# A hybrid-attention and mixture-of-experts layer: gathered rows placed eight partitions apart, expert weights in a ring of six landing pieces and five split pieces

## What is computed

```
scores = sigmoid(xf @ w_router)                    # 512 tokens, 64 experts
idx    = top 8 experts of each token (4 of 8 groups allowed)
wts    = chosen scores / their sum * 2.5
routed = sum over the 8 experts of  wts * (silu(x @ w_gate[e]) * (x @ w_up[e])) @ w_down[e]
shared = (silu(x @ w_gate_s) * (x @ w_up_s)) @ w_down_s
out    = layer_norm(ALPHA * x + shared + routed)
```

## Time and profile before

| | |
|---|---|
| three runs | 1386.76, 1387.98, 1388.95 us; median 1387.98 |
| the profiled execution | 1387.71 us, its span 1385.9 us |
| PE busy | 1311.4 us (95%), 6084 instructions |
| DVE busy | 894.1 us (65%) |
| ACT busy | 709.2 us (51%) |
| POOL busy | 402.5 us (29%) |
| DMA | 311.36 MB, 66971 packets |
| chain that ended last | PE 69%, DMA 22%, ACT 4%, DVE 3% |
| loads of expert weights | 192 x 1 MB, median 11.3 us (gate, up) and 10.8 us (down) from issue to landing |
| gathers, scatters | 64 and 64, median 10.8 us and 9.0 us from issue to landing |

### The profile page before, as it was taken

How to read it: one execution, slowest core, us unless ns; L and a number is a source line. 1 busy time by engine, 2 the same in 40 slices (tenths; PEclk the granted TensorE clock), 3 DMA queues, 4 the chain that set the end, 5 groups by cost and what they waited for, 6 DMA issues and landing times.

```text
span 1385.9 us, 15960 instructions
## 1 busy us (share of the span) xinstructions
PE 1311.4 (95%) x6084; PEld 974.1 (70%) x6084; DVE 894.1 (65%) x1163; ACT 709.2 (51%) x863; POOL 402.5 (29%) x266
## 2 busy tenths in 40 slices
PE   7999999999979999998999999999999999999955
PEld 4989886666656676455587877777777777777722
DVE  4001116655665656465488888888888888888858
ACT  4222323333323321002378888888888888887710
POOL 3232312212232343127233332322222222233204
PEclk9999999999999999998999999999999999999987
DMA  4732201211111151503599999999999999999594
GB/s 161 260 100 74 69 20 57 75 40 39 58 38 58 63 211 38 221 28 125 177 388 359 377 377 363 376 366 369 368 369 371 362 369 373 369 369 373 224 373 180
DMA packets 66971, 311.36 MB, mean 225 GB/s; under 512 B 17660, under 2 KB 17788, under 8 KB 40400
## 3 DMA queue, kind: packets, MB, share of 16 engines
q1 hardware_dynamic: 47408, 276.64, 53.7%
q0 software_dynamic: 19488, 33.70, 6.4%
HBM read 305.74 MB, written 42.01 MB: 251 GB/s over the span
## 4 chain that ended last, share of the span: by engine, by line
PE 69%; DMA 22%; ACT 4%; DVE 3%; issue 1%; POOL 0%; POOLq 0%; SPq 0%; DVEq 0%; ACTq 0%
DMA raw<-in_w_gu 20%; PE PS L651 18%; PE PS L896 9%; PE PS L846 4%; PE PS L849 4%; PE PS L843 4%; PE PS L759 4%; PE PS L707 4%; PE PS L777 4%; ACT w_hi_e L1120 3%; PE PS L730 3%; PE PS L718 2%; DMA parts<-y_d 2%; PE PS L828 2%; PE PS L680 2%; PE PS L679 2%
## 5 line engine op out<-in xcount | busy, mean ns | idle before, releaser
L1436 DVE TENSOR_TENSOR w_lo_e<-raw,w_hi_e 128x2048 fp32r<-128x2048 f32 x192 | 433.8, 2282 | 4.1 <-ACT w_hi_e L1120 4.0
L1120 ACT ACTIVATE w_hi_e<-raw 128x2048 fp32r<-128x2048 f32 x192 | 368.4, 1919 | 113.8 <-DMA raw<-in_w_gu 75.1
L1655 POOL DMA_INDIRECT y_d<-y_slots,tab x64 | 114.2, 1785 | 426.3 <-PE PS L915 284.6
L1607 POOL TENSOR_TENSOR w_lo<-ring,w_hi 128x1024 fp32r<-128x1024 f32 x54 | 128.3, 2376 | 325.7 <-ACT w_hi L1027 325.7
L1280 DVE CUSTOM_DVE_ANT_0 region<-PS,region 128x128 f32<-128x128 f32 (+1 forms) x64 | 30.6, 477 | 183.0 <-PE PS L707 180.9
L846 PE MATMUL PS<-w_hi_e,xs_lo 128*128 128x512 f32 x512 | 144.1, 403 | 0.0
L843 PE MATMUL PS<-w_hi_e,xs_hi 128*128 128x512 f32 x512 | 143.8, 402 | 0.0
L849 PE MATMUL PS<-w_lo_e,xs_hi 128*128 128x512 f32 x512 | 138.7, 393 | 0.0
L1071 ACT ACTIVATE region<-region,nmax 128x128 f32<-128x128 f32 (+3 forms) x80 | 43.6, 546 | 149.7 <-DVE nmax L1280 149.4
L846 PEld LDWEIGHTS PS<-w_hi_e,xs_lo 128*128 128x128 f32 x512 | 91.9, 188 | 32.6 <-DVE xs_lo L1462 15.1
L849 PEld LDWEIGHTS PS<-w_lo_e,xs_hi 128*128 128x128 f32 x512 | 96.1, 188 | 22.3
(11 more groups left out here) (181 smaller groups left out, 2169.5 us busy)
## 6 DMA issues: line engine op xcount, KB each, us to landing
raw<-in_w_gu SPq DMA_DIRECT2D x128, 1024.0 KB, 11.3
raw<-in_w_down_e SPq DMA_DIRECT2D x64, 1024.0 KB, 10.8
ring<-in_w_merge SPq DMA_DIRECT2D x32, 640.0 KB, 3.9
parts<-y_d SPq DMA_DIRECT2D x8, 1536.0 KB, 16.5
ring<-in_w_proj SPq DMA_DIRECT2D x22, 512.0 KB, 3.5
region<-in_w_out SPq DMA_DIRECT2D x1, 4096.0 KB, 14.1
parts<-y_d SPq DMA_DIRECT2D x4, 1024.0 KB, 20.4
bias_d<-bias_rows SPq DMA_DIRECT2D x3, 1280.0 KB, 11.1
```

The source lines that it names most:

```text
L1120: nc.scalar.activation(w_hi_e[b][:, lo:hi], raw[b][:, lo:hi], ACT.Copy).then_inc(made, 1)
L1436: nc.vector.tensor_tensor(w_lo_e[b][:, lo:hi], raw[b][:, lo:hi], w_hi_e[b][:, lo:hi].bitcast(F32), ALU.subtract).then_inc(made, 1)
L1607: nc.gpsimd.tensor_tensor(wl, w, wh.bitcast(F32), ALU.subtract).then_inc(w_lo_made, 1)
L1655: pool.indirect_dma_start(y_d, bass.IndirectOffsetOnAxis(ap=rows, axis=0), y_slots[:, b, :], None, bounds_check=last_row, oob_is_err=False ...
```

## The change

1. **Slots.** The table is read so that slot s = 16 i + j lands in partition 8 j + i (i 0 to 7, j 0 to 15): consecutive slots are eight partitions apart. With 64 tokens, the partitions 8 j + 0 to 8 j + 3 of all 16 j are used. Nothing else of gather and scatter is changed.
2. **Landing.** The 192 pieces of expert weights have one order (`WEIGHTS`: a0 b0 a1 b1 d0 a2 b2 d1 ...; piece n) and land in a ring of six (`LANDED`): four in `raw`, two in the memory of `xT`. `raw` is no longer the memory of `w_lo_e`. From piece 6 on, piece n is loaded once DVE has made the low part of piece n - 6. Pieces 0 and 1 are loaded right behind the shared expert's weights, before the stores of `x1`; pieces 2 and 3 once the shared expert's gate and up are done (they read `xT`); 4 and 5 once `base` has finished (their place is that of `x1`) and `x1` is stored.
3. **Split parts.** `w_hi_e` and `w_lo_e` are rings of five pieces (`SPLIT`). ACT's high of piece n waits for the piece n - 5 to be used by PE.

PE, ACT and DVE keep their order of work.

```diff
+PIECE = GU // 2
+LANDED = 6
+SPLIT = 5
+LAND_AT = (0, 1, 4, 5, 2, 3)
+SPLIT_AT = (0, 4, 1, 2, 3)
+def weight_pieces():
+    order = [("a", 0), ("b", 0)]
+    for e in range(1, N_EXP):
+        order += [("a", e), ("b", e), ("d", e - 1)]
+    return order + [("d", N_EXP - 1)]
...
+        def landing(n):
+            at = LAND_AT[n % LANDED]
+            if at < 4:
+                return raw[:, at, :]
+            return xT[:, :, :].rearrange("p a b -> p (a b)")[:, (at - 4) * PIECE:(at - 3) * PIECE]
...
-            def load_first(e):
-                sp.dma_start(raw[e % 2][:, 0:PART], a["w_gu"][e][:, 0:PART]).then_inc(p0_in[e % 2], 16)
...
+            def load(n):
+                what, e = WEIGHTS[n]
+                if n in (2, 3):
+                    sp.wait_ge(gu_b, QT)
+                elif n in (4, 5):
+                    sp.wait_ge(based, 2 * QT)
+                    sp.wait_ge(x1_stored, 16 * QT)
+                elif n >= LANDED:
+                    sp.wait_ge(lo_made, n - LANDED + 1)
...
+                sp.dma_start(landing(n), weights).then_inc(piece_in[n % LANDED], 16)
...
+            load(0)
+            load(1)
             store_x1(0)
             store_x1(1)
-            sp.wait_ge(mix_done, QT)
-            load_first(0)
-            load_second(0)
-            load_down(0)
             store_x1(2)
             store_x1(3)
...
-            for e in range(1, N_EXP):
-                sp.wait_ge(gu_a, e + QT - 1)
-                load_first(e)
-                sp.wait_ge(gu_b, e + QT - 1)
-                load_second(e)
-                if e >= 2:
-                    sp.wait_ge(y_done, e + QT - 2)
-                    load_down(e - 1)
-            sp.wait_ge(y_done, N_EXP + QT - 2)
-            load_down(N_EXP - 1)
+            for n in range(2, len(WEIGHTS)):
+                load(n)
...
+            def high(what, e):
+                n = PIECE_NO[what, e]
+                act.wait_ge(piece_in[n % LANDED], 16 * (n // LANDED + 1))
+                if n >= SPLIT:
+                    used, by = WEIGHTS[n - SPLIT]
+                    act.wait_ge({"a": gu_a, "b": gu_b, "d": y_done}[used], by + QT + 1)
+                nc.scalar.activation(w_hi_e[:, SPLIT_AT[n % SPLIT], :], landing(n), ACT.Copy).then_inc(hi_made, 1)
...
-            tab_rows = tab_d.rearrange("(c p e) b -> c p e b", p=P, e=N_EXP)
+            tab_rows = tab_d.rearrange("(c i j e) b -> c j i (e b)", i=P // 16, j=16, e=N_EXP)
+            tab_flat = tab[:, :, :].rearrange("p e b -> p (e b)")
```

More of the change, by code:

```diff
@@ L84 @@
         ("q", BR_D): 2052, ("k", BR_D): 2308, ("v", BR_D): 2564, "gates": 2820}
+def weight_pieces():
[3 more added lines that the diff above has]
+    return order + [("d", N_EXP - 1)]
+WEIGHTS = weight_pieces()
+PIECE_NO = {x: n for n, x in enumerate(WEIGHTS)}
 def attention_steps():
@@ L300, in build @@
         last.close()
[L301 to L314, removed]
+        first = ExitStack()
+        first.enter_context(nc.sbuf_tensor("x_nat_from", [P, KT * D], F32))
+        x_nat = first.enter_context(nc.sbuf_tensor("x_nat", [P, QT, D], F32))
+        raw_s = first.enter_context(nc.sbuf_tensor("raw_s", [P, GU + DN], F32))
+        first.close()
+        w_hi_e = sb("w_hi_e", [P, SPLIT, PIECE], F32R)
+        w_lo_e = sb("w_lo_e", [P, SPLIT, PIECE], F32R)
+        x1_area = ExitStack()
+        x1_area.enter_context(nc.sbuf_tensor("x1_from", [P, 2, PIECE], F32))
+        x1 = x1_area.enter_context(nc.sbuf_tensor("x1", [P, QT, D], F32))
+        x1_area.close()
+        raw = sb("raw", [P, 4, PIECE])
+        raw_ov = raw[:, :, :].rearrange("p a b -> p (a b)")
         h_rows = sb("h_rows", [P, 2, FT, P])
@@ L415, in build @@
         slots_clear = sem("slots_clear")
[L416 to L424, removed]
+        sh_in = [sem(f"sh_in{i}") for i in range(3)]
+        piece_in = [sem(f"piece_in{i}") for i in range(LANDED)]
+        hi_made = sem("hi_made")
+        lo_made = sem("lo_made")
         slots_in = [sem(f"slots_in{b}") for b in range(2)]
@@ L821, in gate_up_shared @@
                 if t == 0:
-                    pe.wait_ge((p0_in, p1_in)[part][1], 16)
+                    pe.wait_ge(sh_in[part], 16)
                     pe.wait_ge(var_made, QT - 1)
@@ L832, in gate_up @@
             def gate_up(e, part):
[L834 to L837 removed]
+                b, s, n = e % 2, e + QT, PIECE_NO["ab"[part], e]
+                at = SPLIT_AT[n % SPLIT]
+                wh = w_hi_e[:, at, :].rearrange("p (c n) -> p c n", c=KT // 2)
+                wl = w_lo_e[:, at, :].rearrange("p (c n) -> p c n", c=KT // 2)
+                c0 = part * KT // 2
+                cs = range(c0, c0 + KT // 2)
                 pe.wait_ge(h_made, s - 1)
                 pe.wait_ge(xs_hi_made, e + 1)
[L840 removed]
+                pe.wait_ge(hi_made, n + 1)
                 to = PS[:, G_BANK + s % 2, :]
                 for c in cs:
[L843 removed]
+                    nc.tensor.matmul(to, xs_hi[:, b, c, :], wh[:, c - c0, :], start=(c == 0), stop=False)
                 pe.wait_ge(xs_lo_made, e + 1)
                 for c in cs:
[L846 to L847 removed]
+                    nc.tensor.matmul(to, xs_lo[:, b, c, :], wh[:, c - c0, :], start=False, stop=False)
+                pe.wait_ge(lo_made, n + 1)
                 for c in cs:
[L849 removed]
+                    mm = nc.tensor.matmul(to, xs_hi[:, b, c, :], wl[:, c - c0, :], start=False, stop=(c == KT - 1))
                 mm.then_inc((gu_a, gu_b)[part], 1)
@@ L882, in down @@
             def down(e):
-                b, s = e % 2, e + QT
-                wh, wl = down_of(w_hi_e[b]), down_of(w_lo_e[b])
+                s, piece = e + QT, PIECE_NO["d", e]
+                at = SPLIT_AT[piece % SPLIT]
+                wh = w_hi_e[:, at, :].rearrange("p (t n) -> p t n", t=FT)
+                wl = w_lo_e[:, at, :].rearrange("p (t n) -> p t n", t=FT)
                 pe.wait_ge(hT_made, s + 1)
-                pe.wait_ge(dn_hi, e + 1)
+                pe.wait_ge(hi_made, piece + 1)
                 if e == 0:
@@ L901, in down @@
                 term(hT_hi, wh, True, False)
-                pe.wait_ge(dn_lo, e + 1)
+                pe.wait_ge(lo_made, piece + 1)
                 term(hT_hi, wl, False, False)
@@ L1430, in _, with low @@
             first_norm(1)
-            PART = GU // 2
-            def low(e, lo, hi, ready, made):
-                b = e % 2
-                dve.wait_ge(ready, e + 1)
-                nc.vector.tensor_tensor(w_lo_e[b][:, lo:hi], raw[b][:, lo:hi], w_hi_e[b][:, lo:hi].bitcast(F32),
-                                        ALU.subtract).then_inc(made, 1)
+            def low(what, e):
+                n = PIECE_NO[what, e]
+                at = SPLIT_AT[n % SPLIT]
+                dve.wait_ge(hi_made, n + 1)
+                if n == 2:
+                    dve.wait_ge(gu_a, QT)
+                elif n == 3:
+                    dve.wait_ge(gu_b, QT)
+                elif n == 4:
+                    dve.wait_ge(y_done, QT)
+                nc.vector.tensor_tensor(w_lo_e[:, at, :], landing(n), w_hi_e[:, at, :].bitcast(F32), ALU.subtract)\
+                    .then_inc(lo_made, 1)
             def low_first(e):
-                low(e, 0, PART, p0_hi, p0_lo)
+                low("a", e)
             def low_second(e):
-                low(e, PART, GU, p1_hi, p1_lo)
+                low("b", e)
             def low_down(e):
-                low(e, GU, GU + DN, dn_hi, dn_lo)
+                low("d", e)
             def make_h(s):
```

53 lines of the change are left out of this document (20 added, 33 removed).

## The result

The changed kernel takes 1390.87 us (median of 9 runs, 1388.33 to 1392.1), the kernel before 1387.06 us (9 runs beside them, 1385.91 to 1388.95). The ratio is 1.0026, its 95% interval 1.0017 to 1.0035: 0.26% slower, where 0.4% faster was forecast.

What follows compares the result with a forecast made beforehand. Eight DMA engines full with weights and rows were taken to bound the kernel. Steps of -3.0 and -2.5 us took 1387.98 to 1382.5, stated as 1382.3; its own range 1376 to 1387, the overall range 1367 to 1388.5.

Steps and rivals of the forecast that it cites:

- What bounds the kernel: Expert stretch: eight DMA engines carrying rows are full, 10.01 us of work an expert against 9.96 measured; PE needs 9.45.
- Where the new slots fall: Gathers and scatters: 64 tokens again load eight engines with eight rows each; only the names of the loaded engines change.
- Step 1: Experts 4 to 60: the fullest engine has 7.83 rows on the mean instead of 8; 3.0 us less.
- the head's gain: First experts: the forecast saving from a DMA queue that never empties there, 2.5 us.
- Step 2: Expert weight loads released by DVE instead of PE: nothing in steady state, as more pieces only queue ahead of full engines.
- Step 3: First experts, up to a6's use: the DMA queue never empties, 728.2 against 730.74; 2.5 us less, bounds 0 to 6.1.
- Step 4: First experts: d0 lands late, at 685.7, before ACT takes it at 686.23; hidden, so nothing.
- Steps 5 and 6: Earlier loads of a0 and b0, later ones of a1 and b1, and the kernel's end: nothing from either.
- A: Rival, expert stretch: 64 rows fill 16 engines and PE becomes the bound; about 1357 us, chance 0.12.
- B: Rival, whole kernel: something all engines share sets the pace, rows saved are worth nothing, head's gain given back; 1388, chance 0.11.
- C: Rival, expert stretch: gathers land late behind more queued pieces and PE waits; 150 us slower, 1538, chance 0.05.

Runs made afterwards that it cites:

- e3: The kernel before with slots placed by DMA engine, so that 64 rows are four on each of 16 engines; 1361.53 us, ratio 0.9744.
- e2: The kernel before with the new slots (consecutive slots eight partitions apart), its buffers unchanged; 1396.14 us, ratio 0.9986.
- e14: The changed kernel, its loads also waiting for PE's last use of the same piece two experts earlier; 1384.05 us, ratio 0.998.
- e8: The changed kernel with the old slots, loads also waiting for PE's last use of the same piece two experts earlier; 1386.09 us, ratio 0.9997.
- e11: The changed kernel with the old slots, each load n also waiting for PE's last use of piece n - 7; 1387.88 us, ratio 1.0008.
- e1: The changed kernel with the old slots (slot s in partition s); 1407.91 us, ratio 1.0075.
- e10: The changed kernel with the old slots, where only the loads of d also wait for PE; 1419.82 us, ratio 1.0238.
- e9: e8 with DVE writing low over the landed piece; 1387.41 us, ratio 1.0.
- e6: The changed kernel with the old slots, loads waiting for the low of piece n - 4, at most four under way; 1399.06 us, ratio 1.0084.
- e13: The changed kernel with the old slots, where loads of a and b also wait for PE and d's do not; 1404.34 us, ratio 1.0132.

## Why the prediction was wrong

**What bounds the kernel: right.** The engines with rows set the pace. Spread over 16, the same rows give a kernel in which PE never stops (e3), at 9.35 us for an expert; the forecast took 9.45 for PE alone. "Eight full engines" is a little too even: by the routing of the reference's inputs three of them have 8 rows in every gather and scatter of experts 4 to 60, and the least loaded 6.2 on the mean.

**Where the new slots fall: right.** 64 rows load eight engines before and after, and the slots alone move the time by 0.1% to 0.2% (e2, e14 against e8). The Trainium skill, "DMA: Bandwidth & Descriptors", section "The descriptor swizzle", gave the pairs of quads. This case's traces agree with it for indirect transfers: 64 rows placed by it load 16 engines (e3, 99.9%) and eight apart they load 8 (49.7%).

**Step 1, 3.0 us from the fullest engine's 7.83 rows: neither contradicted nor shown, in a kernel that keeps the old moments.** The 7.83 holds, though fewer rows on the fullest engine come only with the eight experts of 52 tokens or less, and not with every expert under 64. e14's pace is 9.892 against 9.943: 0.051 us for 56 experts, 2.9 us. e2's pace, 9.934, gives only 0.5 us. Single profiled runs are not an interval. The timed ratio of e14, 0.998, is 1.2 to 4.4 us and holds the head's gain as well.

**Step 2, loads released by DVE, "in steady state nothing": this is the step that failed.** The prediction said that "more pieces queue ahead of full engines" and that an earlier issue alone can't change the pace. The first is so (15 us to landing, not the 17 to 20 forecast, and e11 shows that it is harmless). The second is not: DVE's low comes when ACT's copies let it, and SP's issues left their places of 2.2, 5.3 and 8.2 us behind the scatter for 0.8, 4.9 and 8.6. With the old slots that costs 0.75% (e1), 0.19 us for an expert by the pace; with the new ones 1.0026 / 0.998 = 1.0046, which is 6.4 us, and (10.009 - 9.892) x 56 = 6.6 us by the pace. The whole miss is 1390.87 - 1382.3 = 8.6 us, and this term is three quarters of it; against the kernel before, timed beside it, 3.8 us slower came instead of 5.7 faster, and the term is two thirds of those 9.5 us. I had priced the step as a queue of which only the content counts, 10.01 us of work for an expert. That sum was no forecast of the pace to a tenth of a microsecond: kernels with this work ran at 9.94 (before), which already lies under it, and at up to 10.53 us (e10). What makes the engines with rows lose the time stays open.

**Step 3, the first experts, 2.5 us: half right.** ACT takes a6 at 728.80 instead of 730.74:

```profile
728.80 1.92 ACT L1139 ACTIVATE w_hi_e<-raw 128x2048 fp32r<-128x2048 f32 x1 [0.81 <-DMA raw<-in_w_gu]
```

That is 1.9 us. The engines moved 412 GB/s in that stretch, against 421 where weights land alone, which fits a queue that is hardly ever empty, as forecast. But by scatter 4 only 0.8 us of it is left in the changed kernel and 1.5 in e14 (738.51 against 739.97). The rest of the miss is here, and in the spread between profiled runs.

**Step 4, d0 late: nearly as forecast.** ACT takes d0 at 687.16, 0.9 us later than before, and PE stays busy through it:

```profile
687.16 3.92 ACT L1139 ACTIVATE w_hi_e<-raw 128x2048 fp32r<-128x2048 f32 x2
```

**Steps 5 and 6: next to nothing,** as forecast. Scatter 0 comes at 698.92 instead of 699.40, and from scatter 60 to the end of the span pass 89.6 us, 89.1 before.

**The rivals.** A had the right price for its condition (1357, a ratio of 0.978; e3 has 0.9744) and a false condition. B, no change, came nearest to the measured time, but by luck, since its reason, a limit that all engines share near 369 GB/s, falls with e3's 393. C did not happen: gathers land in 10.9 us, 10.8 before. None of the three had the moment of issue in it. Of the 0.07 for slower, C held 0.05; a term for a wait whose releaser moves to another engine, with either sign, was missing.

## What to carry to other kernels

Before slots are spread, find from the bytes of a short transfer which partitions share a DMA engine, and spread over engines, not over partitions: here eight apart was worth 0.1 to 0.2%, and a placing by engine 2.5%. When another engine comes to release the loads, compare the places of their issues against the other transfers, and not their number and depth alone: here, with some four pieces under way, half a microsecond in the place of one load of three, which came with its release by PE instead of DVE, was worth 0.6%, and two loads at once cost up to 2.4%. A ring can keep its buffers and take the old places with one more wait.

## What was not expected of the hardware

- With DMA engines this full, the time depends on the moment of an issue. With the same bytes, and 9 to 15 us between issue and landing, the old slots took from 9.94 us for an expert (e9) to 10.14 (e6). The median over 56 experts moved as the mean did, 9.89 and 10.17, so it is no matter of a few stalls.
- The loss shows between the landings of b and d: 2.8 us where nothing is lost (2.9 in e11), 3.1 in e1, 3.2 in e13, 3.5 in e10. POOL issues the scatter 3.3 to 3.5 us before ACT takes b in all of them.
- A mean DMA share of 0.98 hid that eight of 16 engines had next to no rows, by the prediction's prices a quarter less to do; with the rows on 16 the share was 1.00 and the traffic 24 GB/s higher.
